# Linear attention's value and gate products by Strassen's method in a two-layer streaming encoder

## What is computed

```
def gla_mixer(h, w_in, w_gate_up, b_gate, g_out, w_o):
    z = h @ w_in
    q, k, v, g_lr, r = jnp.split(z, [...], axis=-1)
    log_a = jax.nn.log_sigmoid((g_lr @ w_gate_up + b_gate).astype(f32)) / GLA_TAU
    ...
        o_inter = jnp.einsum('bhck,bhkv->bhcv', qq * jnp.exp(b), S)
        att = jnp.einsum('bhtk,bhtsk,bhsk->bhts', qq, decay, kk)
        o = o_inter + jnp.einsum('bhts,bhsv->bhtv', att, vv)
    ...
    o = rms_norm(o, g_out).astype(h.dtype).reshape(B, L, GLA_NV)
    o = o * jax.nn.silu(r)
    return o @ w_o
```

## Time and profile before

| what | value |
|---|---|
| median of 3 runs | 691.84 us (690.01 to 692.23) |
| profiled execution: its own time | 690.52 us |
| its span in the profile | 688.6 us |
| PE busy | 636.1 us (92%) |
| DVE, ACT, POOL busy | 202.2, 125.8, 46.7 us |
| DMA | 234.00 MB, 340 GB/s over the span |
| mean granted clock of PE | 0.98 of 2.4 GHz |

### The profile page before, as it was taken

The page is one execution under the profiler, slowest core; times in us unless marked ns, Lnnn a source line. Parts: engine busy times, 40 slices in busy tenths (PEclk is TensorE's granted clock), DMA queues, the critical chain, the costliest instruction groups (busy, mean ns, idle before and its releaser), DMA issues.

```text
span 688.6 us, 11565 instructions
## 1 busy us (share of the span) xinstructions
PE 636.1 (92%) x5173; PEld 380.2 (55%) x5173; DVE 202.2 (29%) x466; ACT 125.8 (18%) x282; POOL 46.7 (7%) x73
## 2 busy tenths in 40 slices
PE   7999999999999988998799999999999998678777
PEld 7644775467455635654478544745655553434433
DVE  2137773164122111111145701412731211112102
ACT  2155662011001000000123412221121000000001
POOL 1143100000000000000020600000000000000000
PEclk9999999999999998999999999999999999899799
DMA  9900683948999999999995606649889999999996
GB/s 351 380 37 1 252 360 154 419 186 346 438 430 422 432 427 428 432 428 421 426 426 223 245 1 244 245 200 433 343 354 436 426 433 427 431 426 435 426 420 247
DMA packets 12550, 234.00 MB, mean 340 GB/s; under 512 B 1616, under 2 KB 3152, under 8 KB 3920
## 3 DMA queue, kind: packets, MB, share of 16 engines
q1 hardware_dynamic: 12080, 233.01, 80.5%
q10 hardware_dynamic: 416, 0.18, 0.1%
HBM read 232.14 MB, written 1.05 MB: 339 GB/s over the span
## 4 chain that ended last, share of the span: by engine, by line
PE 73%; DMA 22%; DVE 2%; issue 1%; ACT 1%; another core or an unknown queue 0%; SPq 0%; DVEq 0%
DMA rows<-in_experts 21%; PE ps L1043 11%; PE ps L699 8%; PE ps L1264 8%; PE ps L792 6%; PE ps L1057 5%; PE ps L1083 5%; PE ps L879 4%; PE ps L1253 4%; PE ps L829 3%; PE ps L785 2%; PE ps L819 1%; PE ps L688 1%; PE ps L899 1%; PE ps L912 1%
## 5 line engine op out<-in xcount | busy, mean ns | idle before, releaser
L1043 PE MATMUL ps<-mem,hT 128*32 128x256 f32 x1792 | 106.1, 391 | 15.0 <-DMA mem<-in_experts 14.9
L1043 PEld LDWEIGHTS ps<-mem,hT 128*32 128x32 f32 x1792 | 58.5, 113 | 59.6 <-DMA mem<-in_experts 18.7
L792 PE MATMUL ps<-mem,rows 128*128 128x128 f32 x512 | 67.0, 289 | 6.0 <-issue 5.3
L792 PEld LDWEIGHTS ps<-mem,rows 128*128 128x128 f32 x512 | 62.4, 201 | 11.0 <-issue 8.6
L1977 DVE TENSOR_TENSOR mem<-mem,ps 128x256 f32<-128x256 f32 x16 | 9.7, 608 | 182.3 <-ACT mem L1520 182.3
L699 PE MATMUL ps<-mem,hT 128*128 128x512 f32 x128 | 57.5, 598 | 0.8 <-issue 0.8
L1083 PE MATMUL ps<-hT,mem 128*128 128x512 f32 x120 | 55.7, 606 | 0.3
L1264 PE MATMUL ps<-mem,hT 128*128 128x512 f32 x128 | 56.0, 594 | 0.0
L1057 PE MATMUL ps<-mem 128*32 128x512 f32 x368 | 42.0, 595 | 5.8 <-ACT mem L1524 5.3
L1264 PEld LDWEIGHTS ps<-mem,hT 128*128 128x128 f32 x128 | 24.1, 190 | 29.0 <-issue 28.9
L699 PEld LDWEIGHTS ps<-mem,hT 128*128 128x128 f32 x128 | 23.4, 190 | 28.1 <-issue 28.0
(11 more groups left out here) (336 smaller groups left out, 704.8 us busy)
## 6 DMA issues: line engine op xcount, KB each, us to landing
mem<-in_experts SPq DMA_DIRECT2D x34, 4096.0 KB, 30.5
mem<-in_experts SPq DMA_DIRECT2D x12, 2048.0 KB, 16.1
rows<-in_experts SPq DMA_DIRECT2D x5, 4096.0 KB, 27.1
rows<-in_experts SPq DMA_DIRECT2D x6, 2048.0 KB, 45.2
mem<-in_gla_parts SPq DMA_DIRECT2D x3, 4096.0 KB, 28.5
mem<-in_mla_o SPq DMA_DIRECT2D x1, 4096.0 KB, 29.3
mem<-in_gla_parts SPq DMA_DIRECT2D x2, 2048.0 KB, 46.7
mem<-in_mla_w_in SPq DMA_DIRECT2D x2, 1344.0 KB, 9.9
```

The source lines that it names most:

```text
L792: mm = pe.matmul(spot(k), h[i][:, k * P:(k + 1) * P], Sg[:, i, :], start=first and k % HK == 0, stop=not first, skip_group_check=True)
L1043: mm = pe.matmul(ps[32 * j:32 * j + 32, 2, m * FE:(m + 1) * FE], xe[:, k, 32 * j:32 * j + 32], w[:, j, c * FE:(c + 1) * FE], start=k == 0 ...
```

## The change

The 256x1024 by 1024x1024 product is split into 2x2 blocks: rows by tile (0, 1), the summed dimension by `lower` and `upper` four blocks of 128, the columns by `left` and `right` 512. Seven block products (Strassen's method in Winograd's form) of four matmuls each replace the eight blocks' 32 matmuls, for `v` and for `r`. It needs four sums of row blocks (`row_sums`, 128x512 each, made once by DVE), four sums of weight blocks (`weight_sums`, 128x2048 each; for `v` made by POOL before its differences, for `r` by DVE between its other work), and additions when a product leaves its bank (`evac` of DVE, in place in `gv` and `gr`), after which ACT scales three of the four quarters in SBUF (`scaled`). Products 2 and 5 add into the bank where the product 0 (or 4) before them lies, after that one was copied out.

The weight sums fill slot 2. So `wrr` goes to slot 0 and is loaded after the keys (it was loaded at 345.57 us, with the layer's start), `wgo` to slot 1 after the values, and layer 1's experts start at slot 2 (`FIRST = [0, 4]`), with a new list of the first six loads.

```diff
-    wmo, wv, wrr, wgo = (SLOT[i].rearrange("p (k n) -> p k n", k=KD) for i in (2, 1, 2, 0))
+    wmo, wv, wrr, wgo = (SLOT[i].rearrange("p (k n) -> p k n", k=KD) for i in (2, 1, 0, 1))
-    FIRST = [0, 2]
+    FIRST = [0, 4]
...
-    JOBS += [("v", n, "act", (3, 4, 5, 6, 7)[n]) for n in range(5)] + [("r", n, "act", (4, 5, 6, 4)[n]) for n in range(4)]
+    WHO = ["dve", "dve", "act", "dve", "dve", "dve", "dve"]
+    JOBS += [("v", n, WHO[n], (3, 4, 3, 5, 6, 6, 7)[n]) for n in range(7)] + [("v", 7, "act", 4)]
+    JOBS += [("r", n, WHO[n], (5, 6, 5, 7, 4, 4, 4)[n]) for n in range(7)]
...
-    K_END, V_END, R_END = 14, 19, 23
+    K_END, V_END, R_END = 14, 22, 29
...
+    SUMS = {"v": {1: 5, 3: 5, 6: 5}, "r": {1: 6, 3: 7, 6: 8}}
+
+    def factors(w, n):
+
+        s, t = row_sums, weight_sums
+        return [(hT[:, lower, tile[0]], w[:, lower, left]), (s[1], t[1]), (hT[:, upper, tile[0]], w[:, upper, left]),
+                (s[2], t[2]), (s[0], t[0]), (s[3], w[:, upper, right]), (hT[:, upper, tile[1]], t[3])][n]
...
-        sp.dma_start(SLOT[2], a["gla_parts"][2]).then_inc(w_gr, 16)
         sp.wait_ge(g_job, K_END)
-        sp.dma_start(SLOT[0], a["gla_parts"][3]).then_inc(w_out, 16)
-
-        experts(1, [((0, 1), (g_job, V_END)), ((4, 5), (g_att, 2)), ((2, 3), (g_job, R_END)), ((8, 9), (g_osq, 2)),
-                    ((6, 7), (g_yT, 2)), ((10, 11), (out_done, 12))])
+        sp.dma_start(SLOT[0], a["gla_parts"][2]).then_inc(w_gr, 16)
+        sp.wait_ge(g_job, V_END)
+        sp.dma_start(SLOT[1], a["gla_parts"][3]).then_inc(w_out, 16)
+
+        experts(1, [((2, 3), (g_att, 2)), ((8, 9), (g_job, R_END - 1)), ((0, 1), (g_job, R_END)), ((6, 7), (g_osq, 2)),
+                    ((4, 5), (g_yT, 2)), ((10, 11), (out_done, 12))])
...
+        t1, t2, t3, t4 = weight_sums
+        pool.wait_ge(w_gv, 16)
+        link(pool.tensor_tensor(t1, wv[:, lower, right], wv[:, lower, left], ALU.subtract))
+        link(pool.tensor_tensor(t2, wv[:, upper, right], t1, ALU.subtract))
+        pool.tensor_tensor(t3, wv[:, upper, right], wv[:, lower, right], ALU.subtract)
+        pool.tensor_tensor(t4, wv[:, upper, left], t2, ALU.subtract).then_inc(sums_ok, 1)
         pool.wait_ge(g_decay, 2)
...
-                    i, hb = divmod(n, 2)
                     if n == 0:
                         pe.wait_ge(w_gv if kind == "v" else w_gr, 16)
...
+                    if n in (1, 3, 6):
+                        pe.wait_ge(sums_ok, SUMS[kind][n])
+                    rows, w = factors(wv if kind == "v" else wrr, n)
+                    for k in range(HK):
+                        if (kind, n, k) == ("r", 6, 1):
                             outputs_turned(0)
-                        mm = pe.matmul(b[0:WID[i], :], hT[:, k, COL[i]:COL[i] + WID[i]],
-                                       w[:, k, hb * 512:(hb + 1) * 512], start=k == 0, stop=k == KD - 1)
+                        mm = pe.matmul(b, rows[:, k, :], w[:, k, :], start=k == 0 and n not in (2, 5), stop=k == HK - 1,
+                                       skip_group_check=True)
...
-            job(V_END)
-            job(V_END + 1)
+            for n in range(3):
+                job(V_END + n)
             pe.wait_ge(g_attm, 4)
             scores(1)
-            job(V_END + 2)
+            for n in range(3, 6):
+                job(V_END + n)
             pe.wait_ge(g_attm, 8)
             for m in range(2):
-                pe.wait_ge(*emptied[V_END + m])
+                pe.wait_ge(*emptied[V_END + (5, 2)[m]])
...
+            def scaled(j):
+
+                kind, n, _, _ = JOBS[j]
+                act.wait_ge(*emptied[j])
+                i, cols = {4: (1, right), 5: (0, right), 6: (1, left)}[n]
+                v = (gv if kind == "v" else gr)[:, i, cols]
+                act.activation(v, v, ACT.Copy if kind == "v" else ACT.Silu, scale=rstd[:, i:i + 1]).then_inc(g_act, 1)
...
+                    if n == 0:
+                        ins = dve.tensor_copy(both, b)
+                    else:
+                        dve.wait_ge(*emptied[j - (2 if n == 3 else 1)])
+                        out_, in_ = {1: (both, both), 3: (second, both), 4: (v[:, 1, right], second),
+                                     5: (both, both), 6: (second, second)}[n]
+                        ins = TT(out_, in_, b, ALU.add)
...
+            s1, s2, s3, s4 = row_sums
+            low, up = ([hT[:, ks, tile[i]] for i in range(2)] for ks in (lower, upper))
+            link(TT(s1, low[1], up[1], ALU.add))
+            link(TT(s2, s1, low[0], ALU.subtract))
+            TT(s3, low[0], low[1], ALU.subtract)
+            TT(s4, up[0], s2, ALU.subtract).then_inc(sums_ok, 1)
             dve.wait_ge(g_act, 1)
...
             for i in range(NSUB):
+                if i in (3, 6):
+                    evac(K_END + i // 3 - 1)
                 dve.wait_ge(gk_exp, i + 1)
                 TT(gk[i], gk[i], gkT[:, :, 0:META + SUB * (i + 1)], ALU.mult).then_inc(gk_ok, 1)
+            for n in range(3, 7):
+                evac(K_END + n)
...
+            dve.wait_ge(w_gr, 16)
+            link(TT(t1, wrr[:, lower, right], wrr[:, lower, left], ALU.subtract))
+            TT(t2, wrr[:, upper, right], t1, ALU.subtract).then_inc(sums_ok, 1)
+            dve.wait_ge(g_att, 1)
+            for j in range(4):
+                masked(j)
+            evac(V_END)
+            TT(t3, wrr[:, upper, right], wrr[:, lower, right], ALU.subtract).then_inc(sums_ok, 1)
+            evac(V_END + 1)
...
+            TT(t4, wrr[:, upper, left], t2, ALU.subtract).then_inc(sums_ok, 1)
```

More of the change, by code:

```diff
@@ L441, in build @@
     JOBS += [("a", n, "dve", 3 + n) for n in range(GH)] + [("k", n, "dve", (7 + n) % 8) for n in range(GH)]
-    JOBS += [("v", n, "act", (3, 4, 5, 6, 7)[n]) for n in range(5)] + [("r", n, "act", (4, 5, 6, 4)[n]) for n in range(4)]
+    WHO = ["dve", "dve", "act", "dve", "dve", "dve", "dve"]
+    JOBS += [("v", n, WHO[n], (3, 4, 3, 5, 6, 6, 7)[n]) for n in range(7)] + [("v", 7, "act", 4)]
+    JOBS += [("r", n, WHO[n], (5, 6, 5, 7, 4, 4, 4)[n]) for n in range(7)]
     counts = {"act": 0, "dve": 0}
     emptied = []
-    for _, _, who, _ in JOBS:
-        counts[who] += 1
+    for kind, n, who, _ in JOBS:
+        counts[who] += 4 if (kind, n) == ("v", 7) else 1
         emptied.append(({"act": g_act, "dve": g_dve}[who], counts[who]))
     before_me = [max((i for i in range(j) if JOBS[i][3] == JOBS[j][3]), default=None) for j in range(len(JOBS))]
-    K_END, V_END, R_END = 14, 19, 23
+    K_END, V_END, R_END = 14, 22, 29
+    R_FINAL = [(g_act, counts["act"] + n) for n in (1, 2, 3)]
+    tile = [slice(COL[i], COL[i] + P) for i in range(2)]
+    lower, upper = slice(0, HK), slice(HK, KD)
+    left, right = slice(0, 512), slice(512, D)
+    row_sums = [rows_mem[:, 2 * HALF - 2048 + 512 * i:2 * HALF - 2048 + 512 * (i + 1)].rearrange("p (k n) -> p k n", k=HK)
+                for i in range(4)]
+    weight_sums = [SLOT[2][:, 2048 * i:2048 * (i + 1)].rearrange("p (k n) -> p k n", k=HK) for i in range(4)]
+    SUMS = {"v": {1: 5, 3: 5, 6: 5}, "r": {1: 6, 3: 7, 6: 8}}
[3 more added lines that the diff above has]
+                (s[2], t[2]), (s[0], t[0]), (s[3], w[:, upper, right]), (hT[:, upper, tile[1]], t[3])][n]
     SPREAD = 3
@@ L1314, in gla @@
                         if g == 0:
-                            pe.wait_ge(*emptied[V_END + 2])
+                            pe.wait_ge(*emptied[V_END + 3])
                     elif g == 0:
@@ L1324, in gla @@
                 mm.then_inc(g_o, 1)
-            job(V_END + 3)
+            job(R_END - 1)
             def outputs_ready(i, b):
@@ L1333, in outputs_ready @@
                     pe.wait_ge(w_out, 32)
-                    pe.wait_ge(*emptied[V_END + 3])
+                    pe.wait_ge(*emptied[R_END - 1])
                 pe.wait_ge(g_yT_act, i + 1)
@@ L1405, in copies @@
                 else:
-                    act.wait_ge(q_sums, i)
+                    act.wait_ge(sums_ok, i)
                 act.activation(sq[:, 0:H], q_sb[i], ACT.Square, scale=QK ** -0.5).then_inc(q_squared, 1)
@@ L1560, in evac @@
                 elif kind == "r":
-                    ins = act.activation(gr[:, n // 2, (n % 2) * 512:(n % 2 + 1) * 512], b, ACT.Silu,
-                                         scale=rstd[:, n // 2:n // 2 + 1])
-                elif n == 4:
+                    ins = act.activation(gr[:, 0, left], b, ACT.Silu, scale=rstd[:, 0:1])
+                elif n == 7:
                     for g in range(GH):
@@ L1568, in evac @@
                 else:
-                    i, hb = divmod(n, 2)
-                    ins = act.activation(gv[:, i, hb * 512:(hb + 1) * 512], b, ACT.Copy, scale=rstd[:, i:i + 1])
+                    ins = act.activation(gv[:, 0, left], b, ACT.Copy, scale=rstd[:, 0:1])
                 ins.then_inc(g_act, 1)
+            def scaled(j):
[4 more added lines that the diff above has]
```

(29 more changed lines are left out.)

24 lines of the change are left out of this document (12 added, 12 removed).

## The result

The changed kernel takes 696.15 us (median of 4 runs, 695.26 to 697.18), the kernel before 691.17 beside it (4 runs, 690.01 to 692.23). The ratio is 1.0067, with a 95% interval of 1.0047 to 1.0088: slower by 0.7%, where 696.2 and 0.6% were forecast.

The account below looks back on a forecast made before the run. PE's chain up to layer 1's experts was taken to bound the kernel. -6.9 + 2.5 + 6.8 + 2.0 = +4.4 us, so 696.2 us against the median 691.84 (0.6% slower); range 689.6 to 698.5.

Parts of the forecast that it names:

- 16 rows fewer: PE's value and gate products: 56 instead of 64 matmul rows each for `v` and `r`, saving 6.9 us.
- three new handovers: PE in `v` and `r`: three added waits for a bank's emptying, about 0.82 us each, +2.5 us.
- wait ahead of the third product: PE in the value products: waits for DVE's late copy of the first product out of the same bank, +6.8 us.
- lower clock behind it: PE after its long wait: granted clock at 0.56 for 4.5 us, mostly 1.2 GHz, +2.0 us, with ends 0 and 4.0.
- row sums, DVE's sums for `r`, loads: DVE's row sums, its weight sums in the gate products, and the moved loads: claimed to cost nothing.
- What bounds the kernel: PE's chain up to layer 1's experts sets the end, one to one; behind that the DMA queue never empties.
- The weight sums: POOL's four value sums, 4.45 us each, take turns with DVE's decays: `g_decay` at 386.9 instead of 378.1.
- The sign: Whole kernel: slower 0.70, within 0.3% 0.18, faster by over 0.3% 0.12.
- decay lines that don't exclude POOL: Rival in GLA: only DVE's two-tensor products exclude POOL, wait 2.2 us, clock holds; -2.2 us, 689.6; chance 0.13.
- cheap sums: Rival in POOL's value sums: 3.6 us each, PE waits 3.6 us, clock in doubt; 691 to 693; chance 0.12.
- The third: Rival behind PE's long wait: the clock holds, +2.4 us, so 694.2; chance 0.1.
- the fourth: Rival: more waits than counted, a longer low clock (+2 more) or DVE late with the `r` sums; 698; chance 0.1.

Follow-up runs that it names:

- slots and loads: The kernel before with only the change's slots and, but for one pair, its load order, keeping its own 64-row products: 691.5 us, ratio 0.9993.
- no sums: The changed kernel with POOL's four value weight sums replaced by one memset of eight elements: 688.96 us, ratio 0.9965 to the kernel before.
- memsets: The changed kernel with POOL's four value weight sums replaced by four write-only memsets of about their length: 688.02 us, ratio 0.9943 to the kernel before.
- copy ahead: The changed kernel with DVE's copy of the first value product moved ahead of the query product and multiplications: 695.06 us, ratio 1.0055 to the kernel before.
- all emptyings ahead: The changed kernel with all of DVE's emptyings that PE needs soon moved ahead of or between its multiplications: 688.37 us, ratio 0.9958 to the kernel before.
- wait filled: The changed kernel with 26 unread products put into PE's wait ahead of the third value product: 694.93 us, ratio 1.0055 to the kernel before.
- one handover: The kernel before with the last gate product in bank 5 instead of 4, so the output product needn't wait: 690.72 us, ratio 0.9999.
- without the waits: The changed kernel with emptyings moved ahead, products and banks reordered against back-to-back bank use, one gate sum earlier: 683.5 us, ratio 0.9894 to the kernel before.

## Why the prediction was right

By its terms, on the stretch that grew by 4.79 us (+4.4 forecast):

| term | forecast | measured |
|---|---|---|
| 16 rows fewer | -6.9 | two products of 3.43 us, from start to start: -6.87 |
| three new handovers | +2.5 | 1.0 each: +3.0 |
| wait ahead of the third product | +6.8 | 397.29 - 387.18 - 3.43 = +6.68 |
| lower clock behind it | +2.0 | 5.39 against 3.70: +1.7 |
| row sums, DVE's sums for `r`, loads | 0 | no wait of PE on them; 0 by the run with the loads moved |

The measured terms give +4.5. The 0.3 left over lie behind the waits: the product behind one takes 3.70 instead of 3.60 us, and its successor starts 3.54 us after it (410.33 to 413.87) instead of 3.43. Three products stand behind a wait, and I had not counted that.

The mechanism was right, but that the time came out within 0.1 us of 696.2 is luck. The sum was 0.4 us short on the stretch, and the kernel before took 691.17 us beside the change, where I counted from 691.84; the two nearly cancel. The medians grew by 4.98 us, not by 4.4. Within the sum, too, the handovers (0.5 too cheap) and the clock (0.3 too dear) partly cancel. One reading was off without consequence: the slices that I called 21 to 30 are 22 to 31.

*What bounds the kernel:* right. Every edit in GLA came through to the first read of a half slot, and from there the end follows at a nearly fixed distance:

| run | first value product | first read | stretch | first read to end of span |
|---|---|---|---|---|
| before | 381.90 | 500.90 | 119.00 | 187.7 |
| changed | 383.75 | 507.54 | 123.79 | 187.9 |
| slots and loads | 381.42 | 500.41 | 118.99 | 189.2 |
| no sums | 381.25 | 498.37 | 117.12 | 187.5 |
| memsets | 383.50 | 499.87 | 116.37 | 187.6 |
| copy ahead | 382.88 | 505.47 | 122.59 | 187.5 |
| all emptyings ahead | 381.35 | 497.21 | 115.86 | 187.6 |
| wait filled | 383.57 | 505.70 | 122.13 | 187.8 |
| one handover | 381.95 | 499.88 | 117.93 | 187.8 |
| without the waits | 383.24 | 495.47 | 112.23 | 187.6 |

The one exception, by 1.4 us, is the kernel with two loads the other way round; whether that order is the reason was not tested. The medians move as the stretches do, within 1.1 us: in the last version the stretch fell by 6.77 us and the median by 7.3 (690.77 to 683.5).

*The weight sums:* this term decided, and its chain of turns held. Shifted by the 1.7 us by which this execution was late there (first sum at 364.80 for 363.1), every event lies within 0.2 us of the forecast (in brackets, not shifted): line 2123 ends at 375.06 (373.4 forecast), the third sum at 379.46 (377.7), line 2125 at 380.61 (378.9), the fourth sum at 384.97 (383.2), `g_decay` at 388.66 (386.9), the copy at 397.24 (395.7). Taking the upper price, for two full operands, was right: 4.51 us, 4.45 forecast. POOL's page in the Trainium skill (GPSIMD Engine Reference, 3.1 Elementwise) has 4497 ns for an addition of this size, which the first two sums of this trace (4515 and 4516 ns) confirm within 20 ns.

*Bank handovers:* the right three, each 0.2 too cheap. I read the 0.82 us of "issue" in the chain as the whole cost. From start to start it is more: the products at 410.33 and 442.35 start 7.81 and 7.91 us after the pair of products ahead of them, and a pair takes 6.87 where nothing waits.

*The clock:* the level as forecast, 0.3 us less costly than the 4.5 us at 0.56 gave.

*The sign.* The rivals on the other side needed decay lines that don't exclude POOL (the 5.24 and 6.76 us of line 2123 and the scans exclude that, and the memsets show that POOL's reading is behind it) or cheap sums (4.51 us excludes that). The third, that the clock holds, fell by the profile; that it would have brought about 1.7 us was shown by the filled wait. Of the fourth there is no sign: the second `r` product, which needs DVE's sums, starts 3.5 us after the first (421.97 and 425.50), without a wait.

## What to carry to other kernels

Work that is given to an idle engine isn't free if that engine and a busy one can't read SBUF at the same time: POOL's four sums, 18 us on an engine that idled, delayed DVE's decays by 8.7 us (ready 3.8 us ahead of the first value product before, 4.9 us behind its start now), and PE lost in one wait and the low clock behind it (8.4 us) more than it had saved in `v` and `r` together (6.9 us). When fewer and shorter products depend on each other's emptying, look at the queue of the engine that empties before you look at the arithmetic: here the same arithmetic is 0.7% slower or 1.1% faster than the original, by the order of emptyings, products and banks alone. Moving one emptying ahead only moves the wait to the next bank; move all that the busy engine needs before the long run of other work, and put an independent product between two that share a bank.

## What the runs showed of the hardware

- A long wait costs twice: the idleness of 6.52 us, and then 1.7 us through the clock at 1.2 GHz; a wait of 5.50 us likewise (5.91 us instead of 3.70 for the product behind it, so 2.2). Waits of 0.8 us left the product at 3.70.
- Less contention at one place can be more at another: without sums POOL's differences began 5.55 instead of 3.10 us ahead of DVE's multiplications, and the first three of these took 6.08 instead of 4.80 us.
- While both read SBUF, POOL and DVE took turns, one instruction each, and that for more than DVE's tensor_tensor: a SCALAR_TENSOR_TENSOR of 1.29 us took 5.24 under a sum of POOL, and four scans of 2.57 us together took 6.76. Beside memsets of POOL both took what they take alone.
- A handover of a bank from PE to DVE or ACT and back costs 1.0 us between the starts of two products, of which DVE's copy is 0.68.
